# A residual stream held with features on partitions through three transformer blocks, on one Trainium2 core

## The chip, the cores and the metric

The kernel runs on one NeuronCore of a Trainium2 chip. The metric is the device time of one execution in microseconds. The engines are called by their short names: PE (TensorE), DVE (VectorE), ACT (ScalarE), POOL (GpSimd), SP (SyncE, which issues the DMAs here).

## What is computed

256 tokens of width 1024 pass through three blocks; the residual stream is `h`. The parts that matter are the places where `h` is updated and normalised:

```python
# first block
xn = rmsnorm(h, norm_mix_g)                       # then w_in: attention and a recurrence
h = h + concat(attn, rec) @ w_out
h = h + memory_cross_attention(rmsnorm(h, norm_cross_g), ...)   # w_cq ... w_co
hid = square(relu(rmsnorm(h, norm_mlp_g) @ w_mlp_in))
h = h + hid @ w_mlp_out
h = rmsnorm(h, norm_final_g)
# two further layers, l = 0 and 1
xn = rmsnorm(h, ln_mix[l])                        # then w_in_2: four branches, gates, merge
h = h + (sum_b sigmoid(gate_b) * branch_b @ w_branch_b) @ w_out_2
g, u = split(rmsnorm(h, ln_ffn[l]) @ w_gate_up)
h = h + (silu(g) * u) @ w_down
```

`rmsnorm(x, g) = x * rsqrt(mean(x*x) + 1e-6) * g`. Everything is float32.

## The kernel before

**Products.** Every large float32 product is made as three passes of a reduced type: both operands are split into a high and a low part (`w_hi`, `w_lo`, `x_hi`, `x_lo`, `hid_hi`, `hid_lo`), and PE adds hi by hi, hi by lo and lo by hi in PSUM. All weights come as 192 pieces of 128x2048 floats through a ring of three buffers. For each piece ACT copies the high part (line 1222, called from `split_ahead`, two halves), DVE subtracts it to get the low part (line 1751; line 1758 does one half of a piece), and PE then reads both from one of two slots. All matrix products are issued by the helper on line 552, all transposes by line 671.

**Forms.** In the feature form the weight tile is the stationary operand and the activation (256 tokens) moves, so the result has features on partitions. In the token form the activation is stationary and the weights move, so the result has tokens on partitions. A piece of the feature form, and of the token form of `wout`, `b`, `c`, `v`, is 48 products of 256 columns; `co` (2 pieces), `down` (16) and `wd` (11 in each layer) have 24 products of 512 columns per piece.

**Residual stream.** `h` is held as [128, 2, 1024], tokens on partitions. The products that update it (`wout`, `co`, `down`, `wd`) are in the token form; DVE adds their banks to `h` (lines 1992 to 2006). To normalise, PE transposes `h` (sixteen 128x128 transposes per norm, lines 726 to 732), ACT writes `x_hi` from the transposed banks with the gain (line 1318), DVE writes `x_lo` (line 1870), and only then can the next product start. The sum of squares per token comes from ACT's accumulation along the free dimension (line 1257), and its reciprocal root from DVE on [128, 2] columns (`rsqrt`, lines 1656 to 1667). Where the root is needed along the free dimension, PE spreads it over the partitions (`rstd_row`, line 644) and DVE copies it to `rrow` (line 1941). There are six such norms after the first two, called boundaries here: `wout` to `cq`, `co` to `up`, `down` to `a` of layer 0 (`ln_mix_0`, with the final norm of the first block folded in), `wout` to `gu` in both layers, and `wd` to `a` of layer 1.

**Order.** The order of the work is a list `steps`, written out by hand and read by PE, ACT and DVE alike; each engine runs its own part of each step in order. A step of kind `proj` on ACT and DVE begins with `split_ahead`, which makes the high and low parts of the next piece; a step marked for one engine only does not. The first half of a product of a boundary is read in an order of its own (line 608): all high parts with `w_hi` and `w_lo`, then the low parts, each waiting for a quarter (two feature tiles) of `x_hi` or `x_lo`. A plain product waits for its low weights after 16 of its 48 products. PSUM has banks 0 to 2 for most projections and 3 to 7 for the rest. The order around three boundaries, as DVE has it:

```python
elif name == "co":                                # h += bank; each co piece (line 1995)
elif (name, j) in (("down", 15), ("wd", 10)):     # four adds to h, half a low part after each two
...
for j in range(KT // 2):                          # norm: x_lo from the transposed banks (line 1866)
    ...
if name not in LOADED:
    split_ahead(piece_after[name])                # low parts of the next product and of the one after it
```

In `up`, ACT applies the rectifier and DVE squares (line 2015); in `gu`, DVE scales the gate by `rrow`, ACT applies Silu, DVE multiplies by the up half (line 2026). `down` is scaled by the squared root and `wd` by the root when they are added to `h` (line 2006).

Of the kernel before, what the change touches and what calls it, by code (L numbers as in the profile page):

```python
# [28 lines left out]
ALU = mybir.AluOpType  # L29
# [20 lines left out]
FEATURE = ("u", "y", "q", "k", "ck", "cq", "a", "f", "e", "up", "gu", "gate")  # L50
# [40 lines left out]
R_FINAL = 0  # L91
R_LAYER = D
# [73 lines left out]
def build(nc, x_d, mem_d, xt_d, memt_d, pos_d, const_d, vec_d, row_d, rgw_d, pieces_d, out_d):  # L166
    with ExitStack() as ctx:
# [28 lines left out]
        stat = sb("stat", [P, 512])  # L196
        rrow = sb("rrow", [P, S])
        near = sb("near", [P, 4 * TT, NEAR])
# [10 lines left out]
        x_t = at(A_XT, KT, S)  # L209
# [13 lines left out]
        rope_t = oT[:, 4:6, :].rearrange("p w (i n) -> p w i n", i=2)  # L223

        def col(name, n):
            if name not in cols:
                at0 = sum(k for _, k in cols.values())
                assert at0 + n <= 512, at0
                cols[name] = (at0, n)
            at0, n = cols[name]  # L230
            return stat[:, at0:at0 + n]
# [16 lines left out]
        s_rope_tables, s_ones, s_head_sq, s_factor, s_hg = (sem(n) for n in (  # L248
            "rope_tables_ready", "ones_ready", "head_squares", "lora_norm_factor", "final_gain_applied"))
# [7 lines left out]
        s_norm_low, s_norm_all = sem("norm_low_of_loaded"), sem("norm_high_all")  # L257
        s_sig, s_gate, s_silu = sem("sigmoid"), sem("gate_ready"), sem("silu")
        s_relu, s_hidden_high, s_hidden_low = sem("relu"), sem("hidden_high"), sem("hidden_low")
# [28 lines left out]
        s_h_normed, s_out = sem("h_normed"), sem("out_stored")  # L288
# [69 lines left out]
        def token_weights(w, q, k):  # L358

            c0 = (SLOT + BANK) * (q % SPLITS)  # L360
            return w[:, c0:c0 + PIECE].rearrange("p (k c) -> p k c", k=k)

# [54 lines left out]
        steps += [pe(cq0), act(cq0), ("high", cv1[-1]), pe(cq1), dve(cross("score", 0)), act(cross("score", 0)),  # L417
# [10 lines left out]
        steps += [*ups[:4], ("params",), *ups[4:]]  # L428
        steps += proj("down", js=range(16))
        assert pieces == N_PIECES_1  # L430
        for l in range(L2):
# [4 lines left out]
            steps += [a[0], ("high", f0[-1]), ("low", f0[-1]), ("layerstat", l), a[1], f0, ("finalscale", l)]  # L436
# [18 lines left out]
            for i in range(len(LEVELS) + 1):  # L455
# [13 lines left out]
                if i < 6:  # L469
# [6 lines left out]
            steps += proj("gu", l, range(22))  # L476
# [7 lines left out]
        stats = ["norm_mix_g", "norm_mem_g"] + [n for s in steps if s[0] == "norm" and s[1] not in LOADED  # L484
                                                for n in (["final"] if s[1] == "ln_mix_0" else []) + [s[1]]]
        rs_of = {n: i + 1 - (i > stats.index("final")) for i, n in enumerate(stats)}
# [4 lines left out]
        def norm_input(name):  # L491


            def drained_by(job):
                b, use = jobs[job]
                return drained[b], use + 1

            if name == "norm_mem_g":
                return [(0, tt, 0, D, s_mem, 16) for tt in range(TT)]
            if name == "norm_mix_g":  # L500
                return [(0, tt, 0, D, s_x[tt], 16) for tt in range(TT)]
            if name == "ln_mix_0":
                return [(0, tt, 0, D, s_hg, tt + 1) for tt in range(TT)]
            if name == "norm_mlp_g":
                return [(j, tt, 512 * j, 512, *drained_by(f"co.{j}.{tt}")) for j in range(2) for tt in range(TT)]
            if name in ("final", "ln_mix_1"):
                tag = "down" if name == "final" else "wd0"
                return [(c, tt, 512 * c, 512, *drained_by(f"{tag}.{tt}{c}")) for tt in range(TT) for c in range(2)]
            tag = {"norm_cross_g": "wout", "ln_ffn_0": "wout0", "ln_ffn_1": "wout1"}[name]
            return [(j, tt, 256 * j, 256, *drained_by(f"{tag}.{j}" + "b" * (tag != "wout" and j == 0 and tt == 1))) for j in range(4) for tt in range(TT)]  # L510
# [13 lines left out]
        def _(pe):  # L524
# [119 lines left out]
            def rstd_row(before):  # L644

                pe.wait_ge(s_rs, rs_of[before])
                rs = col("rs." + before, TT)
                bank = fill(f"{before}.rstd", "m")
                for tt in range(TT):
                    ins = mm(bank[:, tt * P:(tt + 1) * P], rs[:, tt:tt + 1].broadcast_to([P, P]), ident, True, True)  # L650
# [63 lines left out]
            for step in steps:  # L714
# [11 lines left out]
                elif kind == "norm" and step[1] not in LOADED:  # L726
                    name = step[1]
                    for j in range(KT // 2):
                        for _, tt, c0, n, s_in, value in norm_input("final" if name == "ln_mix_0" else name):
                            if c0 < 256 * (j + 1) and c0 + n > 256 * j:  # L730
                                pe.wait_ge(s_in, value)
                        turns(f"{name}.{j}", lambda k, tt: h[:, tt, (2 * j + k) * P:(2 * j + k + 1) * P], 2)
                elif kind == "proj":
# [6 lines left out]
                    if before:  # L740
                        def parts(k):
# [5 lines left out]
                            high = s_norm_all, 4 * (norms.index(before) - len(LOADED)) + i + 1  # L747
                            b, use = jobs[f"{before}.{i}.0"]
                            return high, (drained[b], use + 1)
# [36 lines left out]
                    elif name == "co":  # L786
# [3 lines left out]
                        for tt in range(TT):  # L790
                            bank = fill(f"{job}.{tt}", "g")
                            for i in range(2):
                                for kk in range(4):
                                    if j == tt == i == 0:
                                        pe.wait_ge(s_co_high, kk + 1)
                                    elif j == tt == 0:
                                        wait_drained(pe, f"value.cross{kk}")
# [1685 lines left out]
```

## Time and profile before

| | us |
|---|---|
| median of 3 runs | 1214.96 |
| runs, lowest to highest | 1214.29 to 1216.92 |
| profiled execution, its own time | 1215.16 |
| its span in the profile | 1213.0 |
| PE busy | 1200.9 of 1213.0 |
| DVE busy | 842.8 |
| ACT busy | 691.0 |
| DMA | 211.46 MB, 174 GB/s |

The profile covers one execution. Its span is what the profiler recorded; the 2.2 us beside it lie around the recorded instructions. The granted clock of PE is at its upper level (2.4 GHz) in all 40 slices of the page. A product's recorded duration includes its passage through the array, so consecutive products overlap in the rows: their cost is the distance between their starts. On ACT and DVE an instruction that waits for nothing also starts a little before the recorded end of the one ahead of it.

### The profile page before, as it was taken

The numbers are of one execution on the slowest core, as the hardware profiler recorded it, in microseconds if no ns is written. First come the engines' busy times: TensorE is split into PE (matmuls) and PEld (weight loads), VectorE is DVE, ScalarE is ACT, GpSimd is POOL, SyncE is SP. The second block draws the span as 40 slices with busy tenths as digits, with TensorE's granted clock in tenths as the row PEclk, the third lists the DMA queues.
The fourth block names the chain that finished last, engine by engine and source line by source line (L and its number), as shares of the span: only waits on it lengthen the run. The fifth ranks groups of instructions, "written<-read, shape, count | busy, mean of one in ns | idle before, by whom it ended". The sixth has DMA issues, their size and how long they took to land.

```text
span 1213.0 us, 23407 instructions
## 1 busy us (share of the span) xinstructions
PE 1200.9 (99%) x9900; PEld 1126.8 (93%) x9900; DVE 842.8 (69%) x1195; ACT 691.0 (57%) x1150; POOL 40.1 (3%) x88
## 2 busy tenths in 40 slices
PE   8999999999999999999999999999999999999998
PEld 8998989998899999999999998899999989999987
DVE  6997767664476878988756554658789876666544
ACT  5897655553366764793544443557665925544432
POOL 1200100000000000011000000000000100000000
PEclk9999999999999999999999999999999999999999
DMA  9643445565553435433555556534344525455552
GB/s 366 233 146 130 173 143 196 187 209 179 202 174 140 145 135 174 144 137 148 201 185 198 180 203 207 170 145 166 113 174 139 175 105 209 174 187 196 181 203 102
DMA packets 30615, 211.46 MB, mean 174 GB/s; under 512 B 3376, under 2 KB 3760, under 8 KB 5680
## 3 DMA queue, kind: packets, MB, share of 16 engines
q1 hardware_dynamic: 30224, 209.84, 49.3%
q8 instruction: 78, 1.28, 0.4%
q14 instruction: 25, 0.20, 0.0%
q10 hardware_dynamic: 288, 0.14, 0.0%
HBM read 208.92 MB, written 1.05 MB: 173 GB/s over the span
## 4 chain that ended last, share of the span: by engine, by line
PE 86%; ACT 6%; DVE 5%; issue 2%; DMA 1%; SPq 0%; DVEq 0%; ACTq 0%
PE bank L552 84%; ACT w_hi L1222 3%; DVE w_lo L1751 2%; ACT W L1538 2%; PE bank L671 1%; DMA ring<-weight_pieces 1%; PE bank L919 1%; DVE x_lo L1870 0%; DVE stat L2206 0%; ACT W L1222 0%; DVE W L2146 0%; DVE W L2280 0%; ACT W L1509 0%; ACT W L1504 0%; ACT W L1494 0%
## 5 line engine op out<-in xcount | busy, mean ns | idle before, releaser
L1751 DVE TENSOR_TENSOR w_lo<-ring,w_hi 128x2048 fp32r<-128x2048 f32 (+1 forms) x180 | 409.1, 2273 | 238.2 <-ACT w_hi L1222 237.5
L1222 ACT ACTIVATE w_hi<-ring 128x1024 fp32r<-128x1024 f32 (+1 forms) x368 | 366.6, 1047 | 231.7 <-PE bank L552 215.7
L552 PE MATMUL bank<-x_hi,w_hi 128*128 128x256 f32 x1840 | 260.3, 281 | 1.4 <-issue 1.4
L552 PE MATMUL bank<-x_hi,w_lo 128*128 128x256 f32 x1840 | 253.0, 277 | 2.9 <-DVE w_lo L1751 2.9
L552 PE MATMUL bank<-x_lo,w_hi 128*128 128x256 f32 x1840 | 247.4, 277 | 0.2
L552 PEld LDWEIGHTS bank<-x_hi,w_hi 128*128 128x128 f32 x1840 | 230.4, 188 | 5.6 <-ACT x_hi L1222 2.0
L552 PEld LDWEIGHTS bank<-x_hi,w_lo 128*128 128x128 f32 x1840 | 229.0, 188 | 4.2 <-DVE w_lo L1751 3.9
L552 PEld LDWEIGHTS bank<-x_lo,w_hi 128*128 128x128 f32 x1840 | 226.7, 188 | 0.6 <-DVE x_lo L1870 0.6
L552 PE MATMUL bank<-W 128*32 128x32 f32 (+8 forms) x1424 | 81.7, 250 | 3.3 <-issue 1.7
L552 PE MATMUL bank<-w_hi,hid_hi 128*128 128x512 f32 x304 | 76.6, 389 | 0.0
L552 PE MATMUL bank<-w_lo,hid_hi 128*128 128x512 f32 x304 | 76.6, 389 | 0.0
L552 PE MATMUL bank<-w_hi,hid_lo 128*128 128x512 f32 x304 | 76.5, 389 | 0.0
L552 PEld LDWEIGHTS bank<-W 128*32 128x32 f32 (+7 forms) x1424 | 63.0, 135 | 14.1 <-issue 5.0
L552 PEld LDWEIGHTS bank<-w_lo,hid_hi 128*128 128x128 f32 x304 | 57.1, 188 | 11.9
L552 PEld LDWEIGHTS bank<-w_hi,hid_lo 128*128 128x128 f32 x304 | 57.1, 188 | 11.8
L552 PEld LDWEIGHTS bank<-w_hi,hid_hi 128*128 128x128 f32 x304 | 56.8, 188 | 11.7
L552 PE MATMUL bank<-w_hi,x_hi 128*128 128x256 f32 (+1 forms) x400 | 63.2, 288 | 0.0
L552 PE MATMUL bank<-w_lo,x_hi 128*128 128x256 f32 (+1 forms) x400 | 61.7, 284 | 0.0
L1429 ACT ACTIVATE W<-W 128x512 f32<-128x512 f32 x22 | 13.9, 633 | 77.9 <-DVE W L1947 70.5
L1222 ACT ACTIVATE W<-bank 128x512 f32<-128x512 f32 (+2 forms) x60 | 28.7, 505 | 51.4 <-PE bank L552 45.9
L552 PE MATMUL bank<-oT,ring 128*128 128x256 f32 x256 | 57.0, 381 | 0.6 <-DVE xs L2298 0.6
L552 PE MATMUL bank<-w_hi,x_lo 128*128 128x256 f32 (+1 forms) x400 | 56.6, 284 | 0.0
(269 smaller groups left out, 1203.0 us busy)
## 6 DMA issues: line engine op xcount, KB each, us to landing
ring<-weight_pieces SPq DMA_DIRECT2D x191, 1024.0 KB, 4.9
W<-x_features SPq DMA_DIRECT2D x4, 256.0 KB, 4.9
ring<-weight_pieces SPq DMA_DIRECT2D x2, 512.0 KB, 5.9
h<-x SPq DMA_DIRECT2D x2, 512.0 KB, 6.5
W<-rg_weights SPq DMA_DIRECT2D x1, 1024.0 KB, 11.3
xs<-mem_features SPq DMA_DIRECT2D x1, 1024.0 KB, 12.7
oT<-mem SPq DMA_DIRECT2D x1, 1024.0 KB, 14.2
row<-rows SPq DMA_DIRECT2D x1, 1024.0 KB, 8.2
```

Of the source, the lines that this page charges most:

```text
L552: return nc.tensor.matmul(out, lhsT, rhs, start=first, stop=last)
L671: ins = nc.tensor.transpose(bank[0:piece.shape[1], jj * S + tt * P:jj * S + (tt + 1) * P], piece, ident)
L919: ins = nc.tensor.transpose(bank[:, kt * S + qt * P:kt * S + (qt + 1) * P], prob[:, qt, kt * P:(kt + 1) * P], ident)
L1222: return nc.scalar.activation(out, in_, ACT.Copy, scale=scale)
L1429: nc.scalar.activation(product[:, m % 2, :], product[:, m % 2, :], ACT.Silu).then_inc(s_silu, 1)
L1538: ins = nc.scalar.activation(sc[:, qt, :], src[:, qt, :], ACT.Exp, bias=nm[:, qt:qt + 1], scale=token, accum_out=sm[:, qt:qt + 1])
L1751: v.tensor_tensor(whole(w_lo, q), rows, whole(w_hi, q).bitcast(F32), ALU.subtract).then_inc(s_weight_low, 1)
```

## The change

`h` becomes [128, 8, 256], features on partitions, and is loaded from `x_features`; the token copy of `x` is loaded only for its sum of squares. `wout`, `co`, `down` and `wd` take the feature form: `down` and `wd` have 48 products of 256 columns per piece and use all eight PSUM banks, one per feature tile. The transposes of `h` go. For each quarter of `h` ACT writes `x_hi` (or `y_hi`) straight from `h` and squares the quarter into a buffer (`norm_part`); DVE writes the low part (`x_low`) and adds the squares over the quarters (`add_squares`); PE sums over the partitions by a product with ones. Of `cq` the sums are columns (`columns`), of `up` and `gu` they are a 128x256 tile with the same row on every partition (`rows`), on which DVE runs the reciprocal root in eleven instructions. The results of the MLP products are scaled before their high and low parts are made, and no longer when they are added to `h`. `cq`, `up` and `gu` read a second pair of operands `y_hi`, `y_lo` that lies over `xs` and `oT`. The output leaves with features on partitions. The tensors behind the weights move by 80 bytes.

```diff
-FEATURE = ("u", "y", "q", "k", "ck", "cq", "a", "f", "e", "up", "gu", "gate")
+FEATURE = ("u", "y", "q", "k", "ck", "cq", "a", "f", "e", "up", "gu", "gate", "wout", "co", "down", "wd")
...
-        h = sb("h", [P, TT, D])
+        sb("between_rows", [P, 20])
+        h = sb("h", [P, KT, S])
...
+        y_hi = nc.alloc_sbuf_tensor_at("y_hi", [P, KT, S], F32R, offset=nc.sbuf_base - 4 * 2 * KT * S)
+        y_lo = nc.alloc_sbuf_tensor_at("y_lo", [P, KT, S], F32R, offset=nc.sbuf_base - 4 * KT * S)
...
-        steps += [*ups[:4], ("params",), *ups[4:]]
+        steps += [pe(ups[0]), act(ups[0]), ("rows", "norm_mlp_g"), dve(ups[0]), *ups[1:4], ("params",), *ups[4:]]
...
-            steps += [a[0], ("high", f0[-1]), ("low", f0[-1]), ("layerstat", l), a[1], f0, ("finalscale", l)]
+            steps += [a[0], ("high", f0[-1]), ("low", f0[-1]), a[1], ("layerstat", l), f0, ("finalscale", l)]
...
-            steps += proj("gu", l, range(22))
+            gus = proj("gu", l, range(22))
+            steps += [gus[0], ("rows", f"ln_ffn_{l}"), *gus[1:]]
...
+                elif kind == "rows":
+                    pe.wait_ge(s_stat_sum, feature_stats.index(name) + 1)
+                    bank = fill(f"{name}.sum", "m")
+                    full(mm(bank[:, 0:S], ones_col.broadcast_to([P, P]), square_sum[:, 0, :], True, True), f"{name}.sum")
...
-                        if j < count - 1:
+                        if 0 < j < count - 1:
...
+                        else:
+                            wait_low(pe, q)
+                            for m in range(KT):
+                                if j == 0:
+                                    acc.append(fill(f"{tag}{m}", "g" if m < 3 else "m"))
+                                for i in range(3):
+                                    ins = accumulate(m, i)
...
+            def norm_part(name, i):
+                for job in producers(name, i):
+                    wait_drained(act, job)
+                for k in (2 * i, 2 * i + 1):
+                    ins = copy(x[:, k, :], h[:, k, :], gain[:, k:k + 1])
+                ins.then_inc(s_norm_all, 1)
+                if i == 0 and n:
+                    wait_filled(act, f"{feature_stats[n - 1]}.sum")
+                elif i == 3:
+                    act.wait_ge(s_square_added, 3 * n + 1)
+                nc.scalar.activation(square_place(i), h[:, 2 * i:2 * i + 2, :], ACT.Square).then_inc(s_square, 1)
...
-                        if name == "up":
-                            nc.scalar.activation(product[:, m % 2, :], wait_filled(act, job)[:], ACT.Relu).then_inc(s_relu, 1)
...
+            def add_squares(name, i):
+                dve.wait_ge(s_square, 4 * n + i + 1)
+                if stat == "final":
+                    for k in (2 * i, 2 * i + 1):
+                        if k == 0:
+                            link(v.tensor_scalar(rrow[:], src[:, k % 2, :], weight[:, k:k + 1], None, ALU.mult))
+                        else:
+                            link(v.scalar_tensor_tensor(rrow[:], src[:, k % 2, :], weight[:, k:k + 1], rrow[:], ALU.mult, ALU.add))
+                if i:
+                    v.tensor_tensor(square_sum[:], square_sum[:], src, ALU.add).then_inc(s_square_added, 1)
+                    dve.wait_ge(s_square_added, 3 * n + i)
+                if i == 3:
+                    v.tensor_tensor(square_sum[:, 0, :], square_sum[:, 0, :], square_sum[:, 1, :], ALU.add).then_inc(s_stat_sum, 1)
...
+                        x_low(name, 3)
+                        for i in {"norm_mlp_g": (2, 3), "ln_mix_0": range(4), "ln_mix_1": range(4)}.get(name, (3,)):
+                            add_squares(name, i)
+                        split_ahead(piece_after[name])
...
+                elif kind == "rows":
+                    drains(v.tensor_scalar(mean, wait_filled(dve, f"{name}.sum")[:, 0:S], 1.0 / D, EPS, ALU.mult, ALU.add), f"{name}.sum")
+                    wait_drained(dve, f"{name}.sum")
+                    rsqrt(mean, rrow[:], t, S)
+                    if name == "norm_mlp_g":
+                        link(v.tensor_tensor(rrow[:], rrow[:], rrow[:], ALU.mult))
...
                     elif name == "co":
+                        if j:
+                            for i in range(2):
+                                x_low("norm_mlp_g", i)
+                                add_squares("norm_mlp_g", i)
...
                     elif (name, j) in (("down", 15), ("wd", 10)):
+                        for i in range(4):
+                            if i < 2 and done < len(split):
+                                low_half(i)
+                            for m in (2 * i, 2 * i + 1):
+                                drains(v.tensor_tensor(h[:, m, :], wait_filled(dve, job)[:, 0:S], h[:, m, :], ALU.add), job)
+                            if i and after in norms:
+                                if i < 3:
+                                    x_low(after, i - 1)
...
+                        link(v.scalar_tensor_tensor(hidden, bank, 0.0, scaled, ALU.max, ALU.mult))
+                        drains(v.tensor_tensor(hidden, bank, hidden, ALU.mult), job)
...
+                        link(v.tensor_tensor(hidden, hidden, scaled, ALU.mult))
+                        drains(v.tensor_tensor(hidden, bank2(wait_filled(dve, job)), hidden, ALU.mult), job)
```

In the diff `pe` and `mm` are PE's, `nc.scalar` and `act` ACT's, `v` and `dve` DVE's. In `wout` and `co`, `x_low` and `add_squares` of the quarters before stand in the DVE steps in the same way, behind the add to `h` in `wout` and ahead of it in `co`. ACT runs `norm_part` of the early quarters in the `wout` and `co` steps, and the others in the norm step. The scaling by the final norm (`finalscale`) moves from two ACT instructions to eight DVE instructions of 128x256 in front of the piece `kr` of layer 0.

## Rows read from the trace of the kernel before

**Rows 1.** The page: PE's busy time, and the chain that ended last, by engine.

```profile
PE 1200.9 (99%) x9900; PEld 1126.8 (93%) x9900; DVE 842.8 (69%) x1195; ACT 691.0 (57%) x1150; POOL 40.1 (3%) x88
...
PE 86%; ACT 6%; DVE 5%; issue 2%; DMA 1%; SPq 0%; DVEq 0%; ACTq 0%
```

**Rows 2.** Timeline from `co` to `down`: start us, us, engine, line, operation, operands, count.

```profile
163.29 0.39 PE L552 MATMUL bank<-w_hi,x_hi 128*128 128x512 f32 x1
...
168.89 2.06 PE L671 MATMUL bank<-const,h 128*128 128x128 f32 x16
169.09 0.69 DVE L1998 TENSOR_TENSOR h<-bank,h 128x512 f32<-128x512 f32 x1 [0.61 <-PE bank L552]
...
174.14 1.07 PE L552 MATMUL bank<-x_hi,w_hi 128*128 128x256 f32 x8
...
258.46 2.00 PE L552 MATMUL bank<-w_hi,hid_hi 128*128 128x512 f32 x8
...
340.09 0.62 PE L552 MATMUL bank<-w_hi,hid_hi 128*128 128x512 f32 x2
```

**Rows 3.** Timeline, `wout` of the first block to `cq`.

```profile
110.12 1.07 PE L552 MATMUL bank<-w_hi,x_hi 128*128 128x256 f32 x8
...
129.17 1.91 PE L671 MATMUL bank<-const,h 128*128 128x128 f32 x16
...
134.44 1.07 PE L552 MATMUL bank<-x_hi,w_hi 128*128 128x256 f32 x8
```

**Rows 4.** Timeline, `wout` of layer 1 to `gu`; layer 0 has the same pattern.

```profile
1010.05 1.11 PE L552 MATMUL bank<-w_hi,x_hi 128*128 128x256 f32 x8
...
1027.02 1.91 PE L671 MATMUL bank<-const,h 128*128 128x128 f32 x16
...
1032.30 1.07 PE L552 MATMUL bank<-x_hi,w_hi 128*128 128x256 f32 x8
```

**Rows 5.** Timeline, `down` to `a` of layer 0; `wd` to `a` has the same pattern.

```profile
340.35 2.01 ACT L1222 ACTIVATE w_hi<-ring 128x1024 fp32r<-128x1024 f32 x2 [3.43 <-PE bank L552]
...
345.54 2.12 PE L671 MATMUL bank<-const,h 128*128 128x128 f32 x16
...
351.16 1.09 PE L552 MATMUL bank<-x_hi,w_hi 128*128 128x256 f32 x8
```

**Rows 6.** Groups by form on DVE (busy us, mean ns), and one row of its timeline.

```profile
L1751 DVE TENSOR_TENSOR w_lo<-ring,w_hi 128x2048 fp32r<-128x2048 f32 x178 | 408.1, 2293 | 236.4 <-ACT w_hi L1222 235.7
...
L1994 DVE SCALAR_TENSOR_TENSOR h<-bank,h 128x512 f32<-128x512 f32 x10 | 6.9, 692 | 11.6 <-PE bank L552 11.6
...
L1842 DVE SCALAR_TENSOR_TENSOR x_lo<-W,vec,x_hi 128x256 fp32r<-128x256 f32 x8 | 3.3, 479 | 0.0
...
L1704 DVE TENSOR_TENSOR W<-W 128x256 f32<-128x256 f32 x32 | 13.4, 417 | 0.0
...
39.64 0.29 DVE L1799 TENSOR_SCALAR W<-W 128x256 f32<-128x256 f32 x1
```

**Rows 7.** Groups by form on ACT.

```profile
L1222 ACT ACTIVATE w_hi<-ring 128x1024 fp32r<-128x1024 f32 x364 | 365.4, 1055 | 231.7 <-PE bank L552 215.7 <-DMA ring<-weight_pieces 15.6
...
L1222 ACT ACTIVATE hid_hi<-W 128x512 fp32r<-128x512 f32 x38 | 23.5, 618 | 0.7 <-DVE W L2015 0.7
...
L1222 ACT ACTIVATE mem_hi<-xs,vec 128x256 fp32r<-128x256 f32 x4 | 1.7, 497 | 0.0
```

**Rows 8.** Timeline: PE sums over partitions with a ones column, one column each.

```profile
368.09 0.95 PE L552 MATMUL bank<-stat,W 128*128 128x1 f32 x8
...
368.90 5.83 PE L552 MATMUL bank<-ring,W 128*128 128x384 f32 x16
```

**Rows 9.** Timeline: the low part of the first `wd` piece, and its first product.

```profile
714.93 2.29 DVE L1751 TENSOR_TENSOR w_lo<-ring,w_hi 128x2048 fp32r<-128x2048 f32 x1 [2.60 <-ACT w_hi L1222]
...
716.81 2.00 PE L552 MATMUL bank<-w_hi,hid_hi 128*128 128x512 f32 x8
```

**Rows 10.** Timeline: the last DVE instruction before the last output DMA.

```profile
1209.82 0.75 DVE L2006 SCALAR_TENSOR_TENSOR h<-bank,stat,h 128x512 f32<-128x512 f32 x1 [0.61 <-PE bank L552]
```

More of the change, by code:

```diff
@@ L489, in build @@
+        feature_stats = ["norm_cross_g", "norm_mlp_g", "final", "ln_ffn_0", "ln_mix_1", "ln_ffn_1"]
         side_order = [(l, what) for l in range(L2) for what in ("z", "b", "do", "ho")]
[L491 to L503, printed above, removed]
-            if name == "norm_mlp_g":
[L505 to L510, printed above, removed]
@@ L775, in _ @@
                         first_gemm(job, p)
-                    elif name in ("q", "k", "u", "y", "cq", "a", "e", "f"):
+                    elif name in ("q", "k", "u", "y", "a", "e", "f"):
                         gemm(job, "g", p, "feat", parts=parts, between=between)
+                    elif name == "cq":
+                        gemm(job, "g", p, "feat", parts=parts, x_hi=y_hi, x_lo=y_lo, between=between)
                     elif name == "ck":
@@ L784, in _ @@
                     elif name in ("up", "gu"):
-                        gemm(job, "m", p, "feat", parts=parts, between=between)
+                        gemm(job, "m", p, "feat", parts=parts, x_hi=y_hi, x_lo=y_lo, between=between)
                     elif name == "co":
                         q = split_of[p]
-                        hi, lo = (token_weights(w, q, 4) for w in (w_hi, w_lo))
                         pe.wait_ge(s_weight_high, 2 * (q + 1))
[L790 to L797, printed above, removed]
-                                    for w, x in ((hi, x_hi), (lo, x_hi)) if i == 0 else ((hi, x_lo),):
-                                        if w is lo and tt == kk == 0:
-                                            wait_low(pe, q)
-                                        ins = mm(bank[:, :], x[:, kk, tt * P:(tt + 1) * P], w[:, kk, :], i == kk == 0 and w is hi, i == 1 and kk == 3)
-                            full(ins, f"{job}.{tt}")
@@ L1463, in _ @@
                     nc.scalar.activation(at(A_DT, 1024), at(A_ZB, 1024), ACT.Square).then_inc(s_head_sq, 1)
-                elif kind == "finalscale" and step[1] == 0:
-                    act.wait_ge(s_rs, rs_of["ln_mix_0"])
-                    for tt in range(TT):
-                        copy(h[:, tt, :], xs[:, tt, :], col("rs.final", TT)[:, tt:tt + 1]).then_inc(s_h_normed, 1)
                 elif kind == "forget":
@@ L1914, in _ @@
                     v.tensor_scalar(col("rsh0", TT), both[:, 0:TT], 0.5, None, ALU.mult).then_inc(s_rs, 1)
+                elif kind == "finalscale" and step[1] == 0:
+                    gf = V_GAIN + GAINS.index("norm_final_g") * KT
+                    factor = wait_filled(dve, "ln_mix_0.rstd")[:, S:2 * S]
+                    for k in range(KT):
+                        ins = v.scalar_tensor_tensor(h[:, k, :], h[:, k, :], vec[:, gf + k:gf + k + 1], factor, ALU.mult, ALU.mult)
+                    drains(ins, "ln_mix_0.rstd")
                 elif kind == "uscale":
@@ L1932, in _ @@
                     job = job_of(name, l, j)
[L1933 removed]
+                    before = {"ck": "norm_mem_g", "f": f"ln_mix_{l}"}.get(name)
                     if name == "f" and j == 0:
```

358 lines of the change are left out of this document (183 added, 175 removed).

## The prediction

> **What bounds the kernel now.** I read the page first. PE is busy for 1200.9 of 1213.0 us, and 86% of the chain that ended last is PE [rows 1]. So the time is PE's instructions at their pitch plus what PE waits for, and DVE and ACT count only where PE waits for them. Then I read the timeline for the pitch, as starts over counts, and for the stretch at each boundary.
>
> Pitch: from 174.14 to 258.46 there are 93 groups of eight 256-column products, 84.32/744 = 0.1133 us each; from 258.46 to 340.09 fifteen `down` pieces, 81.63/360 = 0.2268 us per 512 columns, twice that; `co` has 5.60/24 = 0.2333 [rows 2]. Token-form `wout` runs at 19.05/168 = 0.1134 in the first block [rows 3] but at 16.97/144 = 0.1178 in a layer [rows 4]. These long stretches hold no stall.
>
> Boundary: from the start of the transposes (PE has finished the product before) to the second half of the next product, whose first half is worth 24 x 0.1133 = 2.72 us: 5.27 us at `cq` [rows 3], 5.25 at `up` [rows 2], 5.28 at `gu` [rows 4], 5.62 at `a` [rows 5]. So a boundary costs 2.5 to 2.9 us, and six of them 16.
>
> **The change, part by part.** Times below count from the end of the last product ahead of the boundary. I use: 0.2 us from a product's end to DVE's start [rows 2]; on DVE 0.69 for 512 columns, 0.42 for 256, 0.48 for the three-operand form with a gain, 0.29 for an operation with a constant, each some 0.08 less where nothing waits and 0.04 more where the next one waits for it, 2.29 for a low part and 1.2 for half of one [rows 6]; on ACT 2.0 for the high part of a piece [rows 5], 0.9 for two 256-column copies, 0.62 for a square of 512 columns [rows 7].
>
> *Form.* `down` and `wd` trade 38 x 24 products of 0.2268 for 38 x 48 of 0.1133: nothing. `wout` in the layers: 2 x 192 x 0.0045 = 1.7 us gained. `co`: 11.2 to 10.9, 0.3 gained. The trace doesn't show the new operands' addresses; the two pitches seen, 0.1133 and 0.1178, bound them from both sides, and I take 0.1133, the one at which 744 products of `up` in this form run [rows 2].
> The Trainium skill, TensorE: Matmul & The Clock Gate, Back-to-back issue gap, charges a warm product N/2.4 ns plus about 2.5 ns; by that 912 additional products would cost 2.3 us more. The pitches in rows 2 show no such fixed part between 256 and 512 columns, so the sum goes by them.
>
> *`wout` to `cq`.* The add to `h` ends at 0.9; ACT copies the last quarter by 1.85. PE has 12 products ready (1.36), waits 0.5, does four (2.3). DVE's low parts are ready at 3.2; PE ends the first half at 3.5. The boundary costs 0.8 where it cost 2.55: gain 1.8. The sums are four instructions, 0.1 each [rows 8]: 0.4. Net gain 1.4. DVE's squares end at 4.3 and the next low part at 6.6; PE wants it at 8.4, so these are hidden.
>
> *`wout` to `gu`, twice.* Same boundary: gain 1.8. The 256-column sum (two instructions) replaces `rstd_row` (four of 128): nothing, covered by no work but equal. Then DVE's root on a full tile: 2 x 0.33 + 9 x 0.46 + 0.46 = 5.3 us, from 6.7 to 12.0. Behind it is queued the low part of `gu` 2, which ends at 14.3; PE wants it at 13.8. With what ripples on (ACT's next high part stands behind Silu) 0.7 lost. Net gain 1.1 each, 2.2.
>
> *`co` to `up`.* The low part of `up` 0 ends at -1.0. Now `x_low` and the squares of quarters 0 and 1 come before the last two adds to `h`: 2 x 0.8 + 0.7 puts those at 1.3 to 2.6. ACT's quarter 3 is ready at 4.25 (before, the last one let PE go at 3.8), the low one at 5.2, PE ends the first half at 5.65: 0.4 lost. The sum 0.3. On DVE follow the squares and their sum to 6.9, the low part of `up` 1 to 9.15, the root and its square 5.7 to 14.8, then `up` 0 itself, two passes, 16.1, and only then the low part of `up` 2, 18.4. PE wants it at 15.95: 2.45 lost. Net loss 3.2. After it DVE spends 4.3 of each 5.44 us (a pass more than now) and catches up.
>
> *`down` to `a` 0.* The half low parts now stand ahead of the adds: high half at -4.1, low half to -2.9, adds to -2.2, second half to -1.1, adds to -0.4, `x_low` 0, adds, `x_low` 1, last add 2.6. ACT's quarter 3 at 3.5, the low one at 4.4, PE ends the first half at 4.9: 0.7 gained. But ahead of the low part of `a` 1 come the weighted squares: from 4.3, eight products with the gain (0.33 + 7 x 0.52), three adds (0.73 each) and one of 0.4: to 10.8. The last square waits for the second add, which holds ACT's high part of `a` 1 until 9.5. Its low part ends at 13.1; PE wants it at 9.4: 3.7 lost. Sums for two norms, eight instructions, 0.8, and four more spreading products, 0.25. Net loss 4.0. The eight `finalscale` instructions (3.2 us on DVE, to 28) lie beside PE's small products behind `kr`, which last to 33; without that cover they would delay the low part of `f` 1.
>
> *`wd` to `a` 1.* The same with no weights: 0.7 gained, low part of `a` 1 at 9.95 against 9.4, 0.55 lost, sums 0.4. Net loss 0.2.
>
> *First `wd` piece, twice.* Its low part ends 0.41 after its first product starts [rows 9]. It was needed only for the third pass; now all of it is awaited first: 0.45 x 2 = 0.9 lost. (`down` 0 has its low part in time.)
>
> *End.* The last add is 256 columns: 0.75 [rows 10] to 0.42, 0.3 gained; four output DMAs of equal size as before. Loading `h` instead of a copy of it, and moving the gain out of the row table, lie in the first 10 us beside loads that are there anyway: nothing; if the cover were gone, under 1 us. SP's queue: a ring buffer is freed by its low part, so the late ones (18.4, 13.1) delay the load of the piece three further on, which is wanted two pieces (10.9 us) after that: covered. POOL's rotary tables no longer wait for the first block's mix and are written to a buffer of their own, long before they are read: nothing.
>
> Sum: gains 1.7 + 0.3 + 1.4 + 2.2 + 0.3 = 5.9, losses 3.2 + 4.0 + 0.2 + 0.9 = 8.3: 2.4 us longer. Against the profiled execution's own 1215.16 (span 1213.0 and 2.2 around it, 0.2 above the median of the runs) that is 1217.5, and 1217.3 against the median. 0.2%, 2.4 us, is about what a measurement of this kernel can tell from no change; so my sum lies at that edge.
>
> **The rivals.** (A) DVE's additions are covered: not slower. Its place is the low part of `up` 2 and of `a` 1, its price the 2.45 and 3.7 us that I put there, and it decides where DVE is ready before 15.95 and 9.4. Against it: some 3 us of my DVE sums would have to be absent. For it: long stretches of DVE's idle time lie next to these places and my sum of small instructions has a margin of a microsecond in each. Time: 1217.3 - 6.2 = 1211.1; half of it absent, 1214.
>
> (B) The pitch of the new products. `wout` shows that the same shapes run at 0.1133 or 0.1178, and I don't know why; the moved tensors and `y_hi`, `y_lo` could land on the second. The 1824 `down` and `wd` products alone: 8.2 us, 1225.5; with `up` and `gu` (2880 x 0.0045 = 13.0) 1238. Against it: `up`, in the feature form, holds 0.1133 over 93 groups [rows 2].
> The Trainium skill, same page, Step-by-step, says that streaming and weight loading have separate SBUF read ports and don't take bandwidth from each other; by that, addresses would not matter, and the two pitches in rows 3 and 4 stay unexplained.
>
> (C) The fixed cost: splitting a 512-column product costs something per product after all. By the difference of `co` per 256 columns from feature products (0.1167 - 0.1133), 912 x 0.0033 = 3.0 us: 1220. The skill's rule above would give 1219.6.
>
> (D) The change doesn't do what it says on the pitch side: `wout` stays at 0.1178 in its new form: 1219.
>
> **How the numbers follow.** My forecast, DVE late twice, has 0.42 and its own range 1214.5 to 1220; A 0.28; B 0.1; C 0.1; D 0.1. The predicted time is 1217.3. The range takes A whole and C, D, and cuts off most of B: 1209.5 to 1224. Faster by over 0.2% (under 1212.5) is most of A, 0.25; within 0.2% is the rest of A and just under half of the forecast, 0.29; slower (over 1217.4) the other half with B, C and D, 0.46.
>
> **What the profile would show.** Line 671 without `h`. Right: boundaries of 3.5 us at `cq` and `gu`, 5.65 at `up`, 4.9 at `a`; PE waiting once for `w_lo` in `up` 2 (about 2.4) and in `a` 1 of layer 0 (3.7), and 0.4 at the first `wd` pieces; groups of eight at 0.907 in `down`. Wrong: no such wait (A), groups of 0.94 where there were none (B), or a wait in a place that I called hidden, as the small products behind `kr` or the cross attention's scores.

## The result, and the profile after

The changed kernel takes 1244.15 us (median of 4 runs, 1243.04 to 1245.22), the kernel before, on the same chip, 1215.15: ratio 1.0236, 95% interval 1.0224 to 1.0248. It is 29 us slower, where I forecast 2.4.

The page of after, its busy times and the chain that ended last (answers to [rows 1]):

```profile
PE 1220.6 (98%) x10782; PEld 1184.2 (95%) x10782; DVE 893.9 (72%) x1271; ACT 674.8 (54%) x1080; POOL 43.8 (4%) x89
...
PE 80%; DVE 9%; ACT 8%; issue 2%; DMA 1%; SPq 0%; DVEq 0%; ACTq 0%
```

PE is busy 19.7 us longer and the chain passes through DVE and ACT for 17% where it was 11%. So there are two things to find: products that take longer, and waits. The timeline of after, on PE (start us, us, engine, line, operation, operands, count), shows the first (answers to [rows 2, 4]):

```profile
193.67 1.12 PE L551 MATMUL bank<-y_hi,w_hi 128*128 128x256 f32 x8
...
266.82 1.11 PE L551 MATMUL bank<-y_hi,w_lo 128*128 128x256 f32 x8
267.77 0.40 PE L551 MATMUL bank<-hid_hi,w_hi 128*128 128x256 f32 x2
268.01 0.40 PE L551 MATMUL bank<-hid_lo,w_hi 128*128 128x256 f32 x2
...
1047.96 1.07 PE L551 MATMUL bank<-x_hi,w_hi 128*128 128x256 f32 x8
1048.86 1.07 PE L551 MATMUL bank<-x_lo,w_hi 128*128 128x256 f32 x8
```

From 193.67 to 266.82 lie 77 groups of eight: 73.15/616 = 0.1188 us per product of `up`, without one stall; before, the same shape in the same form took 0.1133. `down` takes 0.2355 for two, 0.1178 each. But `wout` of a layer, in its new form, runs at 0.90/8 = 0.113. What differs in these rows is the operand: `y` and `hid` are slow, `x` is fast.

The second thing: the waits, then the granted clock by stretches (length, PE busy and products, PEclk, DMA share, GB/s) at three places of after:

```profile
171.07 0.39 PE L551 MATMUL bank<-y_hi,w_hi 128*128 128x256 f32 x1 [1.95 <-ACT y_hi L1228]
...
172.39 0.58 PE L551 MATMUL bank<-y_hi,w_hi 128*128 128x256 f32 x1 [0.58 <-ACT y_hi L1228]
...
188.26 0.97 PE L551 MATMUL bank<-y_hi,w_lo 128*128 128x256 f32 x6 [1.83 <-DVE w_lo L1756]
...
371.29 1.21 PE L551 MATMUL bank<-x_hi,w_lo 128*128 128x256 f32 x8 [1.97 <-DVE w_lo L1756]
```

```profile
168.00:172.00 4.00, 1.86 (x14) 1.00 0.79 262
172.00:176.00 4.00, 3.61 (x18) 0.57 0.00 0
...
188.00:192.00 4.00, 3.74 (x21) 0.67 0.65 233
192.00:196.00 4.00, 4.00 (x32) 0.90 0.75 246
...
800.00:804.00 4.00, 2.57 (x18) 0.97 0.68 246
804.00:808.00 4.00, 4.00 (x24) 0.60 0.00 0
```

The waits are at the places that I forecast. What I had not: behind three of the stretches with stalls (`up` 0, `up` 2, `a` of layer 1) the granted clock falls from 2.4 to 1.2 GHz and comes back some 3.4 us later (twice the loss of 1.7 us). Each fall costs about 4.00 x (1 - 0.57) = 1.7 us, all three 5.1 by these rows. They are rows of the slowest of the four executions (1245.22 us, mean clock 0.996); the others have 0.997, 0.997 and 0.999. The kernel before, in its profiled execution, has no stretch of 4 us below 1.00 up to its last products.

### The profile page after: what moved, and what is told of

It reads as the page before. It is cut to its first block, busy times and chain, and to the rows that moved or that the text cites. A ratio compares the mean times of both kernels' runs of the same rounds, so it can differ in the third digit from the quotient of the medians.

```text
span 1243.4 us, 25122 instructions
## 1 busy us (share of the span) xinstructions
PE 1220.6 (98%) x10782; PEld 1184.2 (95%) x10782; DVE 893.9 (72%) x1271; ACT 674.8 (54%) x1080; POOL 43.8 (4%) x89
## 4 chain that ended last, share of the span: by engine, by line
PE 80%; DVE 9%; ACT 8%; issue 2%; DMA 1%; SPq 0%; DVEq 0%; ACTq 0%
PE bank L551 78%; ACT w_hi L1228 3%; DVE w_lo L1756 3%; ACT W L1543 1%; DMA ring<-weight_pieces 1%; PE bank L927 1%; PE bank L671 1%; DVE stat L2257 0%; ACT x_hi L1228 0%; ACT W L1228 0%; DVE w_lo L1763 0%; DVE W L2197 0%; DVE W L2331 0%; DVE rrow L1668 0%; DVE square_part L1667 0%
## 5 line engine op out<-in xcount | busy, mean ns | idle before, releaser
L551 PE MATMUL bank<-x_hi,w_hi 128*128 128x256 f32 x1072 | 160.1, 284 | 5.3 <-ACT x_hi L1228 2.9
L551 PE MATMUL bank<-x_hi,w_lo 128*128 128x256 f32 x1072 | 153.3, 278 | 4.7 <-DVE w_lo L1756 4.7
L551 PE MATMUL bank<-y_hi,w_hi 128*128 128x256 f32 x992 | 144.2, 284 | 3.5 <-ACT y_hi L1228 3.5
L551 PE MATMUL bank<-x_lo,w_hi 128*128 128x256 f32 x1072 | 145.3, 278 | 0.0
L551 PE MATMUL bank<-y_hi,w_lo 128*128 128x256 f32 x992 | 142.3, 282 | 1.9 <-DVE w_lo L1756 1.8
L551 PE MATMUL bank<-y_lo,w_hi 128*128 128x256 f32 x992 | 139.8, 283 | 0.1
L551 PEld LDWEIGHTS bank<-y_hi,w_hi 128*128 128x128 f32 x992 | 129.8, 190 | 4.7 <-ACT y_hi L1228 4.5
L551 PEld LDWEIGHTS bank<-x_lo,w_hi 128*128 128x128 f32 x1072 | 133.3, 189 | 0.0
L551 PEld LDWEIGHTS bank<-y_hi,w_lo 128*128 128x128 f32 x992 | 128.7, 189 | 2.5 <-DVE w_lo L1756 2.5
L551 PEld LDWEIGHTS bank<-y_lo,w_hi 128*128 128x128 f32 x992 | 127.9, 190 | 0.5 <-DVE y_lo L1787 0.3
```

The lines of the kernel that those rows point to most:

```text
L551: return nc.tensor.matmul(out, lhsT, rhs, start=first, stop=last)
```

## The experiments

**1. The pitch by place, alone, and the change with the arena moved.** `e1_map` holds only the products, one source line for each place. The places are bytes in a partition: `x_hi` begins at 16544, `y_hi` at 99520, `hid_hi` at 115904 (before: 115808), `w_hi` at 57696. So the tensors behind the weights moved by 96 bytes, not by the 80 given ahead of the prediction: the 20 floats of the filler `between_rows` take up the next multiple of 32 bytes, and a filler of 16 or 28 floats puts them 32 bytes lower or higher.

> This kernel leaves the whole computation out: it fills the SBUF with one piece of data and then issues the products of the changed kernel alone, on TensorE only, each group of 96 from another place of the moving (or stationary) operand, the weights where both kernels have them. It reads the pitch of 128x256 products by place. In the changed kernel the products on x_hi/x_lo come every 0.1134 us, those on y_hi/y_lo every 0.1188, those of down and wd on hid_hi/hid_lo every 0.1178. Theory P (place): the pitch hangs on the byte offset of the operand in a partition. y_hi lies at a multiple of 64 bytes, x_hi 32 bytes beyond one. Then the group on x's place shows about 0.1134 and that on y's place about 0.1188 with no other engine at work, and moving y by +32 or -32 bytes gives 0.1134. Theory T (traffic): the pitch is set by what ScalarE and VectorE read and write beside the products; then all places show the same pitch, 0.1134. Theory R (role): weights held still and hid moving is slower than the reverse whatever the place; then the feature-form groups of hid show 0.1178 at both kernels' places and at +32 and +64.

Its timeline on PE: L42 `y`'s place, L43 to L46 `y` moved by -96, -64, -32 and +32 bytes, L74 and L75 `x` and `y` again (L76, the next group, ends L75):

```profile
41.07 11.55 PE L42 MATMUL bank<-big 128*128 128x256 f32 x96
52.46 11.52 PE L43 MATMUL bank<-big 128*128 128x256 f32 x96
63.82 11.45 PE L44 MATMUL bank<-big 128*128 128x256 f32 x96
75.11 11.06 PE L45 MATMUL bank<-big 128*128 128x256 f32 x96
86.01 11.53 PE L46 MATMUL bank<-big 128*128 128x256 f32 x96
...
395.52 11.04 PE L74 MATMUL bank<-big 128*128 128x256 f32 x96
406.40 11.55 PE L75 MATMUL bank<-big 128*128 128x256 f32 x96
417.80 11.06 PE L76 MATMUL bank<-big 128*128 128x256 f32 x96
```

Start to start, over 96: `x` 10.88/96 = 0.1133, `y` 11.40/96 = 0.1188, exactly the two pitches of the kernels, with every other engine idle and the DMAs moving 1 GB/s. So traffic is not needed for it. Of 35 places, those 32 bytes beyond a multiple of 128 had 0.1132 to 0.1139 (the very first group left out: 0.144 on `x`'s place, for a reason that its rows, at a granted clock of 1.00, don't show; the repeat is L74), wherever in the SBUF (eleven regions 16 KB apart); those at 64, 96 and 0 had 0.1188, 0.1184 and 0.1176. `y_hi` lies at 64. The period is 128 bytes, not the 64 of my theory: +32, which theory P called fast, was slow, and -32 was fast. `hid` moving in the feature form had 0.1179 to 0.1192, but none of their four places was at 32, so they did not decide about the role.

> The changed kernel with the filler in front of h 8 floats larger: h, y_hi, y_lo and the arena (with hid_hi, hid_lo and mem_hi) all lie 32 bytes further on, at 32 beyond a multiple of 64 bytes, as x_hi does. Nothing else changes. Theory P (place): the pitch of cq, up and gu goes from 0.1188 to 0.1134 and that of down and wd from 0.1178 to about 0.1134, which takes 2880 x 0.0054 + 1824 x 0.0044 = 15.6 + 8.0 = 23.6 us off: 1220.5 us. Theories T (traffic of the other engines) and R (role of hid): no change, 1244 us within 1.

```
-        sb("between_rows", [P, 20])
+        sb("between_rows", [P, 28])
```

1243.36 us, ratio 1.0229 (1.0213 to 1.0245): nothing gained. The shift put `y` and `hid` at 96, which the map shows as 0.1184; in this kernel's own timeline `y` has 0.1184 too (216 products of `up` from 191.39 to 216.97). By theory P as stated this was a miss; by the map it had to be.

**2. Two steps of VectorE reordered.** In this kernel the first piece of `up` is scaled by a factor row that isn't made yet; the work is the same.

> The changed kernel with two steps of VectorE reordered and no work changed: the low part of the weights of up 2 is made before the reciprocal root on the full tile, and at ln_mix_0 and ln_mix_1 the low part of a's second piece is made before the last two additions of squares. Theory W (waits): at co->up the wait of 1.83 us for w_lo and the stretch at a granted clock of 0.66 behind it go (some 3.5 us), at both starts of a layer the wait of 2.0 us shrinks to about 1 and the slow stretch behind it shortens: 5 to 8 us in all, 1237.5 us. Rival theory: the products behind these waits find the next step late instead (the row of factors for up, the sums for the statistics), and the time stays within 2 us of 1244.

```
-        steps += [pe(ups[0]), act(ups[0]), ("rows", "norm_mlp_g"), dve(ups[0]), *ups[1:4], ...
+        steps += [ups[0], ("rows", "norm_mlp_g"), *ups[1:4], ...
                         for i in {...}.get(name, (3,)):
+                            if name[:6] == "ln_mix" and i == 2:
+                                split_ahead(piece_after[name])
                             add_squares(name, i)
```

1241.13 us, 3.0 less: under theory W's 5 to 8, over the rival's 2. Between the two profiled executions (1245.22 and 1240.70) it is 4.5 us, of which 3.4 are the clock: it falls once (at 172) in place of three times. The waits for `w_lo` went from 7.1 to 5.0 us, while others grew (issue 2.9 to 4.0). Two of its other executions had a clock of 0.997, one 1.000: the falls come or don't on small differences. At the start of layer 1 PE stands still here as it did in after (two waits of 0.71 us), without a fall.

**3. Absolute place or relation; the change at the fast place.**

> Products alone again, the computation left out. The first map showed 0.1133 us for a 128x256 product whose moving operand begins 32 bytes beyond a multiple of 128 (x_hi's place in both kernels), and 0.1188, 0.1184 and 0.1176 at 64, 96 and 0 beyond one; the weights lay at 96 beyond one throughout. This kernel moves the weights and the data apart: each of 4 x 4 places modulo 128 bytes, for feature form, token form and token form with 512 columns; then feature form on x_hi's place, on 32 bytes beyond it, and token form, first alone and then with ScalarE and VectorE copying and subtracting elsewhere in the SBUF. Theory A (absolute): only the data's own offset counts: the four columns of the table repeat for every place of the weights. Theory B (relation): the difference of the two offsets counts, so the fast place of the data moves with the weights: data at 0, 32, 64, 96 is fast with weights at 64, 96, 0, 32. Theory C (both): only the pair 32 and 96 is fast. For traffic: if the other engines' reads and writes slow the products, the last groups show more than 0.1133 on x_hi's place; I expect 0.1133 there, within 0.0005.

Feature form, pitch in us from the starts in its timeline (data and weights moved by so many bytes from `x_hi`'s and `w_hi`'s places):

```
             data +0   +32     +64     +96
weights +0   0.1133  0.1186  0.1185  0.1175
        +32  0.1174  0.1135  0.1186  0.1184
        +64  0.1184  0.1176  0.1135  0.1185
        +96  0.1188  0.1185  0.1176  0.1136
```

Theory B holds for the feature form: it is the difference of the two offsets that counts, fast where the weights begin 64 bytes beyond the data, modulo 128 (0.1133 to 0.1136). In token form with 256 columns only the pair +0, +0 was fast (0.1133; the rest 0.1173 to 0.1201), so there the difference alone does not decide. With 512 columns two of 16 pairs were fast (0.2269, the rest 0.2325 to 0.2342), the two in which weights and data agree modulo 256; so do the kernel before's `w_hi` and `hid_hi` (57696 and 115808), which fits the 0.2268 of its `down`: in `e1_map` 512 columns had 0.2267 with `hid` at that place and 0.2342 at 115904. With ScalarE and VectorE at work elsewhere (L78 for L77, L80 for L79, L82 for L81 below: `x`'s place, 32 bytes beyond, token form):

```profile
580.07 21.94 PE L77 MATMUL bank<-big 128*128 128x256 f32 x192
601.85 22.95 PE L79 MATMUL bank<-big 128*128 128x256 f32 x192
624.64 21.94 PE L81 MATMUL bank<-big 128*128 128x256 f32 x192
...
657.49 21.92 PE L78 MATMUL bank<-big 128*128 128x256 f32 x192
679.25 22.95 PE L80 MATMUL bank<-big 128*128 128x256 f32 x192
702.04 21.94 PE L82 MATMUL bank<-big 128*128 128x256 f32 x192
```

21.76/192 = 0.1133 with them against 21.78/192 = 0.1134 without: their traffic costs nothing. The DMAs moved 1 GB/s in both, so this says nothing of theirs.

> The changed kernel with the filler in front of h 4 floats smaller, 16 for 20: h, y_hi, y_lo and the arena with hid_hi, hid_lo lie 32 bytes earlier, at 32 beyond a multiple of 128 bytes, where x_hi lies. Nothing else changes. By the first map cq, up and gu go from 0.1188 to 0.1133 and down and wd from 0.1178 to 0.1133: 2880 x 0.0055 + 1824 x 0.0045 = 15.8 + 8.2 = 24.0 us off, 1220.1 us, within 2 of my forecast of 1217.3 plus what the clock took (theory P, place). Should the place matter only while the other engines are idle, as in the map, the time stays near 1243.

```
-        sb("between_rows", [P, 20])
+        sb("between_rows", [P, 16])
```

1222.18 us, ratio to the kernel before 1.0066 (1.0053 to 1.0078): four floats of unused space are worth 22.0 us (20.7 by the two ratios), where 24.0 were expected. PE's busy time did fall by 24.0 (1220.6 to 1196.6); but its waits for `w_lo` grew from 7.1 to 8.5 us and those on issue from 2.9 to 4.2, which gives 2.7 back. (The expectation's 2880 products leave out `cq`; with it `y` has 2976.) Its timeline from `up` to `down`, to be read against that of after:

```profile
261.13 1.07 PE L551 MATMUL bank<-y_hi,w_hi 128*128 128x256 f32 x8
262.04 1.07 PE L551 MATMUL bank<-y_lo,w_hi 128*128 128x256 f32 x8
262.94 1.07 PE L551 MATMUL bank<-y_hi,w_lo 128*128 128x256 f32 x8
263.85 0.39 PE L551 MATMUL bank<-hid_hi,w_hi 128*128 128x256 f32 x2
264.08 0.39 PE L551 MATMUL bank<-hid_lo,w_hi 128*128 128x256 f32 x2
```

Groups of eight follow after 0.90 or 0.91, pairs after 0.23. `hid` as the moving operand, with its weights held still, is as fast as any: theory R falls. The clock's three falls are still there (mean 0.996).

> The kernel with the filler of 16 floats and the two reorderings of VectorE: the low part of up 2's weights ahead of the reciprocal root on the full tile (the first product of up still scaled behind the root), and the low part of a's second piece ahead of the last two additions of squares. The reorderings alone took 3.0 us off the changed kernel (1244.15 to 1241.1). If the two causes add, the time is that of the filler alone less 3: 1217. If a faster pitch leaves VectorE later than before at the same places, the waits come back and it stays at 1219 to 1220. It is not expected to beat the kernel before (1215) by more than the measurement tells.

1221.25 us, ratio 1.0054 (1.0041 to 1.0068): no more than 0.9 below the filler alone. It missed both figures. Ahead of the root it asked for the low part of the second piece of `up`, which was made already, so nothing moved there; at both layers ScalarE's last square waited for an addition and held the high part of `a` 1 behind it until 356.60:

```profile
356.06 0.63 ACT L1281 ACTIVATE square_part<-h 128x512 f32<-128x512 f32 x1 [3.50 <-DVE square_sum L1804]
356.60 1.99 ACT L1228 ACTIVATE w_hi<-ring 128x1024 fp32r<-128x1024 f32 x2
```

**4. Order by what PE wants next, and what the clock costs.**

> The kernel with the filler of 16 floats (1222.2 us) and another order of the same work on VectorE and ScalarE around three boundaries. co->up: h's addition for the last products of co stands ahead of y's low parts and of the additions of squares, so that y_hi's last quarter comes about 1.9 us earlier; the low parts of up 3 and up 4 (counted from 1) stand ahead of the first scaled product. Into both layers: the four additions into h stand ahead of x's low parts, ScalarE makes the four high parts without squares between them and the high part of a's second piece ahead of the last squares, VectorE that piece's low part ahead of the last additions of squares. Theory W (waits and the clock behind them): the first half of up goes from 6.6 to about 4.1 us with no fall of the clock (4 us off), up 3's wait of 2.1 us and the fall behind it go (3.8 off), the first half of a loses 1.3 us at each layer and the waits and the fall behind them go (2 x 1.3 + 2.8 + 1.7): 1222.2 - 14 would be the most; I expect 9 to 12 off, 1211.5, which would beat the kernel before. Rival: the sums come late for the statistics and the gain is 3 to 6 us, 1217.

```
 # co, on DVE: h's addition first
-                        if j:
-                            for i in range(2):
-                                x_low("norm_mlp_g", i)
-                                add_squares("norm_mlp_g", i)
                         for mp in range(2):
                             ... h += bank ...
+                            if j:
+                                x_low("norm_mlp_g", mp)
 # last down / wd piece, on DVE: only low_half and the additions to h
-                                if i < 3:
-                                    x_low(after, i - 1)
 # ln_mix_*, on ACT: part 0, square 0, parts 1 2 3, high part of a 1, squares 1 2 3
 # ln_mix_*, on DVE: x_low 0 to 3, add_squares 0, low part of a 1, add_squares 1 2 3
-... act(ups[0]), ("rows", "norm_mlp_g"), dve(ups[0]), ...
+... act(ups[0]), ("high", ups[2][-1]), ("low", ups[2][-1]), ("rows", "norm_mlp_g"),
+    ("high", ups[3][-1]), ("low", ups[3][-1]), dve(ups[0]), ...
```

1211.89 us, as expected (1211.5), and 10.3 less than with the filler alone (11.9 by the ratios, as the kernel before measured 1.4 us slower beside it), ratio to the kernel before 0.9968 (0.9956 to 0.9981): it beats both kernels, by 0.3% and 2.6%. Between 163 and 195 us the trace has two waits of PE over 0.25 us:

```profile
169.00 0.38 PE L551 MATMUL bank<-y_hi,w_hi 128*128 128x256 f32 x1 [0.62 <-ACT y_hi L1228]
193.65 1.20 PE L551 MATMUL bank<-y_hi,w_lo 128*128 128x256 f32 x8 [0.68 <-DVE w_lo L1767]
```

Up to the last products no stretch of 4 us is below a clock of 0.99, and all five executions have a mean of 1.000.

> The kernel with the filler of 16 floats (1222.2 us), with TensorE kept busy where it waited: 15 and 4 products of zeros with y_hi (each 128x256, which add nothing to the open sum) ahead of the waits of 1.99 and 0.48 us in up 1, 16 ahead of the wait of 2.12 us in up 3, 5 and 5 ahead of the waits of 0.7 us in a 1 of both layers. The waits end when they did, as the products issued before them take no longer than they lasted. Theory K (clock): the granted clock fell to 1.2 GHz for some 3.3 us behind three stalls (171 to 175, 188 to 192, 789 to 793 us), each worth about 1.7 us; with the products in the stalls it stays at 2.4 GHz and the time falls by 3 x 1.7 = 5 us to 1217.1. Rival: the clock falls for another reason than the stalls, and the time is 1222 or, by the added products, up to 1 us above.

```
+                def keep(k):
+                    for _ in range(hold.get(k, 0)):
+                        mm(bank[:, 0:n], zero.broadcast_to([P, P]), x_hi[:, 0, :], False, False)
```

1223.23 us: no gain in the median. The profiled execution (1220.86) had a clock of 1.000, the other four (1223.07 to 1223.47) 0.997; and in the profiled one a wait on issue of 2.44 us at 551.76, which the one with the filler alone has not at that place, took most of the rest back. By the median the expectation's rival is right (1222, up to 1 us above); and in four of five executions the clock was low although the stalls were filled, for a reason that no trace shows. Inconclusive, so I put the question again with one stall in an otherwise quiet kernel:

> The reordered kernel (1211.9 us) with VectorE's old order at co->up alone: y's first two low parts and the addition of squares ahead of h's additions for co's last products. Theory K: the stalls of up 1 come back (1.99 and 0.5 us for 0.6, so 1.9 more), and behind them the clock falls to 1.2 GHz for some 3.3 us, which costs 1.7 more: 1215.5. Without a fall (rival: stalls alone cost only their own length) 1213.8.

> The kernel with the old order at co->up and, in its stalls alone, 16 and 4 products of zeros (128x256, added to the open sum). The waits end when they did. Theory K: the granted clock stays at 2.4 GHz, and only the price of the clock is saved, 1.7 us against the run without them: 1213.8 for 1215.5. Rival (the clock falls by something else, or the added products delay as much as they save): 1215.5 or above.

The first (`e9_stall`) takes out the `co` part of the edit of `e7_order`; the second (`e10_filled`) adds `keep` at `up` 0 (16 and 4), and the column of zeros. With the stall, then with it filled, the clock by stretches:

```profile
168.00:172.00 4.00, 1.99 (x10) 0.76 0.42 178
172.00:176.00 4.00, 4.00 (x20) 0.50 0.00 0
176.00:180.00 4.00, 4.00 (x31) 0.89 0.63 195
```

```profile
168.00:172.00 4.00, 3.69 (x30) 1.00 0.46 193
172.00:176.00 4.00, 4.00 (x35) 1.00 0.02 4
176.00:180.00 4.00, 4.00 (x37) 1.00 0.52 166
```

Medians of 11 runs each: 1216.16 and 1213.42 us, ratios to the kernel before 1.0005 (0.9997 to 1.0014) and 0.9981 (0.9972 to 0.9990). All eleven executions with the products of zeros had a clock of 1.000, ten of the eleven without had 0.996 to 0.999. The one execution without them whose clock was 1.000 took 1213.84, as long as those with them. So what the stall costs beyond its length comes with the fall, and theory K holds. Its size is 2.7 us for the 1.7 expected. In the profiled execution with the stall the clock stayed down twice as long as in after, which costs up to 4 x (0.24 + 0.50 + 0.11) = 3.4, and the two profiled executions differ by 3.2 (1215.70 and 1212.53). But the median one had a mean clock of 0.999, which is 0.6 to 1.8 us, so part of the 2.7 stays unaccounted. The stalls themselves cost the other 1.5 us or so (1213.42 - 1211.89).

> The reordered kernel with the filler of 20 floats, as the change has it: only the place goes back, the order stays. If place and order are independent, the 22.0 us that the filler of 16 took off come back: 1211.9 + 22.0 = 1233.9. If the slower products had covered VectorE's lateness at the boundaries, the difference is smaller, down to 19.

1234.03 us, ratio 1.0155 (1.0139 to 1.0170): 22.1 us above `e7_order`, as the filler alone gave 22.0. By the ratios it is 22.7 against 20.7: place and order are independent within some 2 us.

## Why the prediction was wrong

The sum closes with two terms that it did not have: 1217.3 forecast, + 22.0 for the place (measured), + 5.1 for the clock (by rows of after) = 1244.4; measured 1244.15. That it closes to 0.3 us is partly luck: the place is 20.7 by the ratios, and the 5.1 are those of the execution with the lowest clock.

**Form: the step that failed.** "I take 0.1133, the one at which 744 products of `up` in this form run." The pitch did not belong to the form. It belonged to the distance between `x_hi` and `w_hi`, and the change gave `cq`, `up` and `gu` another operand at another place and moved the arena (the region with `hid_hi` and `hid_lo`). What the runs showed in its place: 0.1178 for `down` and `wd`, 0.1188 for `cq`, `up` and `gu`, together 22.0 us. The prediction said that the trace doesn't show the new addresses; the kernels do. The upper bound 0.1178, set by the nearest rows, was right for `down` and `wd` and too low for `y`. Rival B named the mechanism, but at 0.1 and with its two parts apart; with both, 1238, it was the nearest case, and outside the stated range (up to 1224). The argument against it, that `up` holds 0.1133 over 93 groups, spoke of `x_hi`, which `up` no longer reads. The Trainium skill's sentence on separate read ports (TensorE: Matmul & The Clock Gate, Step-by-step) stood in the prediction against B; `e1_map`, in which nothing but the data's place differs, shows 4.8% between two places, so for these products (float32 in the rows, fp32r in the kernel) the measurement decides against reading it as "addresses would not matter".

Rival C is void: at the right place 256 columns take half of 512 (0.1133 and 0.2268). The fixed 2.5 ns of the Trainium skill (TensorE: Matmul & The Clock Gate, Back-to-back issue gap) don't show in these pitches.

**Clock: not in the sum.** I costed each stall at its own length. Behind three of them the clock fell, 1.7 us each by the rows of after; the clean pair of runs gave 2.7 for one.

**The boundaries came as forecast.** `cq` is 3.75 us to its second half (forecast 3.5), `gu` 3.6 (3.5), `a` 0 4.8 (4.9). `up` took 7.1 for 5.65 and the first piece of `a` in layer 1 5.9 for 4.9; both hold a fall of the clock.

**DVE late twice: right.** In `a` 1 of layer 0 the low part of the weights ended 13.0 us behind the last product (forecast 13.1) and PE's third pass began 3.6 late (3.7). In `up` 2 it ended at 20.2 (forecast 18.4) but PE, slowed by the boundary, waited 1.83 for 2.45. So rival A, that DVE's additions are covered, was wrong. They could be taken off PE's path by order alone, which neither the sum nor a rival had; `e7_order` shows it, and with the clock that went with them it was worth 10.3 us. At the two first `wd` pieces PE waited 0.6 together (forecast 0.9).

**Rival D was wrong but for a quarter**: in the layers the second to fourth piece of `wout` went to 0.1133, as the sum had it. The first piece of each layer did not, though it reads the same two operands in the same form; its two halves take turns, product by product:

```profile
588.70 0.40 PE L551 MATMUL bank<-x_hi,w_lo 128*128 128x256 f32 x2
...
592.23 2.05 PE L551 MATMUL bank<-x_lo,w_hi 128*128 128x256 f32 x16
594.12 1.11 PE L551 MATMUL bank<-x_hi,w_hi 128*128 128x256 f32 x8
```

These are 46 products in 5.42 us, 0.1178 each. So the distance of the two offsets is not all that sets the pitch.

Left open: why the distance of two operands modulo 128 bytes matters at all; what else sets the pitch in that first piece; why `wout`, `b` and others of the kernel before ran at 0.1178 in token form though `e4_map2` gives 0.1133 for that place; and what makes a fall of the clock come in one execution and not in the next.

## What to carry to other kernels

A pitch read from a trace belongs to a pair of operands at their addresses. When a change moves a buffer or gives a product another one, price all its products at the slower pitch seen, at least (here 0.1178 was seen and 0.1188 came); the term is large: 4800 products by 5 ns. Before believing such a kernel slow, try the filler in front of the moved buffers in steps of 32 bytes. And an engine's late step costs more than its wait if TensorE's clock falls behind it: put on VectorE and ScalarE first what TensorE wants next (additions to `h`, high parts), and sums for statistics last.

## What the hardware showed that I had not expected

- In `e4_map2` 128x256 products of fp32r operands, weights held still, took 0.1133 to 0.1136 us where the weights lie 64 bytes beyond the moving data modulo 128, and 0.1174 to 0.1188 elsewhere. With the weights moving, 512 columns took 0.2269 where the two agree modulo 256 and 0.2325 to 0.2342 elsewhere, and 256 columns 0.1133 at one of 16 pairs.
- The penalty is there with every other engine idle (0.1188 in `e1_map`), and VectorE and ScalarE at full work add nothing (0.1133 with them, 0.1134 without).
- Stalls of 2.0 and 0.6 us a few products apart were followed by a stretch at 1.2 GHz; with products of zeros in them the clock stayed at 2.4 GHz, and the kernel with the useless work was 2.7 us faster than the one that only waited.
